# Three edits to a two-block fp32 kernel: the first mixture's loop written out on TensorE, the input rows on another queue, and zeros written elsewhere

## The reference

```python
def reference(x, ...):
    # first block, two layers
    x = x + even_mixer(rms_norm(x))       # differential attention beside a gated recurrence
    x = x + swiglu(rms_norm(x))           # dense, 2816 wide
    x = x + pool_mixer(rms_norm(x))
    x = x + moe_swiglu(rms_norm(x))       # "first mixture": 8 experts, 3584 wide, top 2 of 8
    x = rms_norm(x)
    # second block, one layer, with a context of 256 tokens
    x = x + mod[2] * hybrid_mixer(...)    # delta rule and gated linear attention, both directions
    x = x + mod[5] * hier_moe(...)        # "second mixture": 4 groups of 8 experts, 512 wide
    return rms_norm(x)

def moe_swiglu(t, ...):
    top_val, top_idx = top_k(t @ router_w, 2)
    gates = softmax(top_val)              # combine[:, e]: the gate of expert e, or 0
    for e in range(8):
        he = silu(t @ wg[e]) * (t @ wu[e])
        out = out + (combine[:, e:e + 1] * he) @ wd[e]
```

## Time and profile before

| | |
|---|---|
| median of 3 runs | 2699.87 us (2699.5 to 2700.07) |
| profiled execution, its own time | 2700.57 us |
| its span | 2698.8 us |
| TensorE matmul busy | 2468.5 us, 91% of the span |
| VectorE, ScalarE, GpSimd busy | 616.5, 379.6, 157.3 us |
| granted TensorE clock, mean | 0.963 of full speed |
| HBM read | 671.98 MB, 249 GB/s over the span |

### The profile page before, as it was taken

The page is one execution under the profiler, slowest core; times in us unless marked ns, Lnnn a source line. Parts: engine busy times, 40 slices in busy tenths (PEclk is TensorE's granted clock), DMA queues, the critical chain, the costliest instruction groups (busy, mean ns, idle before and its releaser), DMA issues.

```text
span 2698.8 us, 52755 instructions
## 1 busy us (share of the span) xinstructions
PE 2468.5 (91%) x24386; PEld 1591.9 (59%) x24386; DVE 616.5 (23%) x1160; ACT 379.6 (14%) x619; POOL 157.3 (6%) x145
## 2 busy tenths in 40 slices
PE   7778999799999999999999898899889889999997
PEld 5536776556556656655565678895567544444443
DVE  1451001201000000101010356741542232222223
ACT  1121101100000000000000333213241100000001
POOL 1000000000000000000000024520210000000000
PEclk9889999799999999999999999999999989999998
DMA  8484332599989999998999300022021459999995
GB/s 297 170 297 157 125 140 80 208 393 351 393 306 393 351 340 356 350 393 312 393 351 367 138 1 1 1 94 94 32 94 60 152 225 400 399 399 401 401 401 205
DMA packets 273260, 676.26 MB, mean 251 GB/s; under 512 B 5891, under 2 KB 9438, under 8 KB 268830
## 3 DMA queue, kind: packets, MB, share of 16 engines
q1 hardware_dynamic: 270624, 666.91, 65.7%
q0 software_dynamic: 2112, 6.04, 0.7%
q10 hardware_dynamic: 318, 0.10, 0.0%
HBM read 671.98 MB, written 1.05 MB: 249 GB/s over the span
## 4 chain that ended last, share of the span: by engine, by line
PE 76%; DMA 11%; DVE 6%; ACT 3%; issue 2%; SPq 2%; POOL 1%; DVEq 0%; ACTq 0%; POOLq 0%
PE ps L621 25%; PE ps L712 22%; PE ps L733 11%; DMA ring<-in_w_exp_up 10%; PE ps L797 5%; PE ps L965 3%; ACT arena L2017 2%; SPq L567 2%; PE ps L1098 1%; PE ps L1110 1%; PE ps L719 1%; PE ps L1108 1%; PE ps L695 1%; POOL arena L2475 1%; PE ps L944 1%
## 5 line engine op out<-in xcount | busy, mean ns | idle before, releaser
L712 PE MATMUL ps<-ring,arena 128*32 128x256 f32 x10752 | 598.0, 382 | 16.7 <-issue 15.4
L712 PEld LDWEIGHTS ps<-ring,arena 128*32 128x32 f32 x10752 | 349.0, 111 | 249.7 <-issue 32.1
L621 PE MATMUL ps<-hT,ring 128*128 128x256 f32 (+1 forms) x1792 | 443.1, 408 | 20.1 <-ACT arena L2017 7.3
L2017 ACT ACTIVATE arena<-ps 128x384 f32<-128x384 f32 (+5 forms) x312 | 165.9, 552 | 1830.0 <-PE ps L712 581.3
L621 PEld LDWEIGHTS ps<-hT,ring 128*128 128x128 f32 x1792 | 345.6, 193 | 121.1 <-issue 68.3
L733 PE MATMUL ps<-ring,arena 128*32 128x256 f32 x5376 | 300.5, 379 | 0.0
L797 PE MATMUL ps<-ring,arena 128*64 128x512 f32 x1024 | 233.8, 611 | 29.0 <-DMA ring<-in_w_exp_up 26.1
L733 PEld LDWEIGHTS ps<-ring,arena 128*32 128x32 f32 x5376 | 173.9, 110 | 115.3 <-issue 1.3
L1441 DVE TENSOR_TENSOR arena<-arena,ps 128x384 f32<-128x384 f32 x56 | 31.0, 554 | 825.2 <-ACT arena L2017 825.2
L797 PEld LDWEIGHTS ps<-ring,arena 128*64 128x64 f32 x1024 | 81.1, 141 | 178.5 <-issue 178.5
L621 PE MATMUL ps<-arena 128*128 128x128 f32 (+1 forms) x1064 | 133.7, 287 | 15.9 <-ACT arena L2017 5.1
(11 more groups left out here) (360 smaller groups left out, 1844.3 us busy)
## 6 DMA issues: line engine op xcount, KB each, us to landing
ring<-in_moe_wg SPq DMA_DIRECT2D x56, 2048.0 KB, 11.3
ring<-in_moe_wu SPq DMA_DIRECT2D x56, 2048.0 KB, 16.3
ring<-in_moe_wd SPq DMA_DIRECT2D x56, 2048.0 KB, 17.2
ring<-in_w_exp_gate SPq DMA_DIRECT2D x32, 2048.0 KB, 17.5
ring<-in_w_exp_up SPq DMA_DIRECT2D x32, 2048.0 KB, 18.8
ring<-in_w_exp_down SPq DMA_DIRECT2D x32, 2048.0 KB, 15.2
ring<-in_w_in SPq DMA_DIRECT2D x13, 2048.0 KB, 10.5
ring<-in_w_ada SPq DMA_DIRECT2D x12, 2048.0 KB, 10.5
```

Source lines behind the costliest of these rows:

```text
L621: last = mm(outp, l, r, start=(i == 0), stop=(i == n - 1))
L712: last = mm(flat[32 * q:32 * q + 32, S * r:S * r + S], x_[:, k, 32 * r:32 * r + 32], gu[:, :, k, q * P:(q + 1) * P], start=(k == 0), stop= ...
L2017: return nc.scalar.activation(*a, **k)
```

## The change

It has three parts.

1. The input's two token tiles are two DMAs at the head of SyncE's queue, each with a semaphore of its own, ahead of the first weights; ScalarE's first norm waits for tile 0 and tile 1 separately. GpSimd's queue begins with `table`.
2. In the first mixture's round that is always run, TensorE's loop over four passes is written out as eight experts, with constant semaphore values. The other engines' loops stay.
3. GpSimd zeroes `ysb` and `GcT` right after the linear attention's output is ready (`og_ready` 2), ahead of the wait for `res_ready` 6. `facc` is zeroed by ScalarE, as two copies of 128 x 1024 of `table` with scale 0, behind the copy of `frow`; VectorE waits for it before the second mixture's round.

```diff
--- before.py
+++ after.py
@@ -582,11 +582,14 @@
                         sp.wait_ge(*at("m2_dn", r * PAIRS + PAIRS))
                         sp.sem_inc(sem("rounds_streamed"), 1)
 
+            for t in range(NT):
+                sp.dma_start(res[:, t, :], ins["x"][0, t * P:(t + 1) * P, :]).then_inc(inc("x%d_in" % t), 16)
             before = [None] * NSLOT
             for i in range(len(plan)):
                 if i == 1:
                     sp.wait_ge(*at("rows_in", 16 * (len(ROWS_A) + len(ROWS_B))))
-                    sp.wait_ge(*at("x_in", 16))
+                    sp.wait_ge(*at("x0_in", 16))
+                    sp.wait_ge(*at("x1_in", 16))
                     sp.wait_ge(*at("table_in", 16))
                 load(i, before[i % NSLOT])
                 before[i % NSLOT] = plan[i][4]
@@ -747,9 +750,13 @@
                     down(U1 - 1)
 
                 gather(0, 0)
-                with pe.Fori(0, E1 // 2) as p:
-                    for b in range(2):
-                        expert(2 * p + b, b, R * UNITS + 2 * U1 * p + U1 * b, U1 * p)
+                if x == "m":
+                    for e in range(E1):
+                        expert(e, e % 2, U1 * e, U1 * (e // 2))
+                else:
+                    with pe.Fori(0, E1 // 2) as p:
+                        for b in range(2):
+                            expert(2 * p + b, b, R * UNITS + 2 * U1 * p + U1 * b, U1 * p)
                 scatter(E1, 0)
 
             def pairs_round(x, R):
@@ -1993,6 +2000,7 @@
             done(last)
             route(2, E2, C2, lgt, gprob)
             ve.wait_ge(*at("m2_zeroed", 1))
+            ve.wait_ge(*at("facc_zeroed", 1))
 
             def copy2(x_):
                 C = P
@@ -2134,7 +2142,7 @@
                 ac.dma_start(rowsB[o:o + n, :], v.rearrange("(r d) -> r d", d=P)).then_inc(inc("rows_in"), 16)
 
             functions(LN)
-            norm(0, res, [("x_in", 16)] * 2)
+            norm(0, res, [("x0_in", 16), ("x1_in", 16)])
             ac.wait_ge(*at("cols_ready", 1))
             gained(hTx, colA("ln_mix_even", 0, 8), "hT_act")
             ac.wait_ge(*at("lam_dot", 1))
@@ -2367,6 +2375,9 @@
             gained(hTx, gM, "hT_act", mod[:, 24:32, 0])
             ac.wait_ge(*at("grow_sum", 2))
             done(act(frow.rearrange("p (a b) -> p a b", a=2), ps[:, 4:6, :], ACT.Copy), "frow_ready")
+            for t in range(NT):
+                last = act(facc[:, t, :], table[:, 0:D], ACT.Copy, scale=0.0)
+            last.then_inc(inc("facc_zeroed"), 1)
             gdf = oh2[:, :, 0:4]
             ac.wait_ge(*at("grp_shift", 1))
             done(act(gdf, gdf, ACT.Exp), "grp_exp")
@@ -2379,7 +2390,6 @@
         @block.gpsimd
         def _(po):
             G = nc.gpsimd
-            po.dma_start(res[:, :, :], ins["x"][0].rearrange("(t p) d -> p t d", p=P)).then_inc(inc("x_in"), 16)
             po.dma_start(table[:, :], ins["k_table"]).then_inc(inc("table_in"), 16)
             po.dma_start(const1, ins["k_table1"]).then_inc(inc("table1_in"), 16)
             for i, name in enumerate(("lam_q1", "lam_q2", "lam_k1", "lam_k2")):
@@ -2475,15 +2485,15 @@
                     G.tensor_tensor(W2[l % 2].rearrange("p h (n c) -> p (h n) c", c=2 * b), g_, mid, ALU.subtract)\
                         .then_inc(inc("Wd_ready"), 1)
 
+            po.wait_ge(*at("og_ready", 2))
+            G.memset(ysb, 0.0)
+            G.memset(GcT[:, 1, :, :], 0.0).then_inc(inc("m2_zeroed"), 1)
             po.wait_ge(*at("res_ready", 6))
             with nc.allow_non_contiguous_dma(reason="router columns"):
                 po.dma_start(wre[:, :, 0:4], ins["w_router_grp_2"][0].rearrange("(k p) n -> p k n", p=P)).then_inc(inc("router2_in"), 16)
                 po.dma_start(wre[:, :, 4:36], ins["w_router_exp_2"][0].rearrange("(k p) n -> p k n", p=P)).then_inc(inc("router2_in"), 16)
             po.dma_start(brt[:, 0:4], ins["b_router_grp_2"].to_broadcast([P, 4])).then_inc(inc("router2_in"), 16)
             po.dma_start(brt[:, 4:36], ins["b_router_exp_2"].to_broadcast([P, 32])).then_inc(inc("router2_in"), 16)
-            G.memset(facc, 0.0)
-            G.memset(ysb, 0.0)
-            G.memset(GcT[:, 1, :, :], 0.0).then_inc(inc("m2_zeroed"), 1)
             po.dma_start(glrow, ins["g_final_2"][None, :].to_broadcast([P, D])).then_inc(inc("glrow_in"), 16)
```

## The result

The changed kernel takes 2681.31 us (median of 4 runs, 2678.46 to 2682.54), the kernel before in the same comparison 2699.97 (4 runs, 2699.5 to 2700.84). The ratio is 0.9929, 95% interval 0.9912 to 0.9946: faster by 18.7 us. The forecast was 2675.1 with a range of 2672.4 to 2678.8, so the sign was right and the time 6 us too low, outside the range. The profiled execution after took 2680.94 us, with a span of 2679.1 (before: 2698.8). All of the following differences are taken between these two spans, which are 19.7 us apart.

The account below looks back on a forecast made before the run. TensorE's matmuls were taken to bound the kernel (76% of the chain of waits, DMA 11%). Loop 22.3, start 2.2 and zeros 0.3 us made 24.8 us off 2699.87: forecast 2675.1 us, range 2672.4 to 2678.8.

Parts of the forecast that it names:

- the loop's term: First mixture, TensorE's loop written out: 15.4 us idle plus 6.9 us at the low clock, 22.3 us gained.
- As after the change TensorE has no gap there to cool in: First mixture: the first groups of experts 3, 5 and 7 run at 10.36 us, gaining 6.9 us.
- C: First mixture: the wait at the turn isn't the branch's but belongs to each second expert; 2697.4 us, chance 0.05.
- D: First mixture: TensorE's code, four times as long, is fetched too late in the straight run; up to 2709.9 us, chance 0.03.
- E: First mixture: another engine's loop keeps part of the turn, a third of 22.3 us stays; 2682.5 us, chance 0.04.
- the start: Input rows first on SyncE's queue: the norm starts 2.41 us earlier; 2.2 us taken, between 1.8 and 2.4.
- Rival B: Kernel start gives nothing, as x lands near 11.5 or the table or small rows come late; 2677.3 us, chance 0.12.
- the zeros: Second router: without memsets transposes start 2.3 us earlier, but TensorE waits for router DMAs; 0.3 us gained, ends 0 and 2.3.
- of the 2.3 us 0.2 are left, and with the matmuls' own lead-in 0.3: Second router: TensorE, there at 2154.7, waits till 2156.75 for the last router DMA, leaving 0.3 us gain.
- rival A: Second router: the router columns don't bind, so the memsets' whole 2.3 us come in; 2673.1 us, chance 0.12.
- the sum: Whole kernel: 22.3 + 2.2 + 0.3 = 24.8 us less than the median 2699.87, forecast 2675.1 us.
- a microsecond taken from TensorE's path counts: Whole kernel: outside the second mixture's loads DMA binds only the very start, so TensorE savings shorten the total.

Follow-up runs that it names:

- The two versions with the early columns: Zeros moved and the second router's four column and bias DMAs issued some 100 us earlier: on the kernel before 2697.49 us, on the changed kernel 2675.38 us.

## Why the prediction missed

**Right: the loop's term.** 22.3 us were forecast for the mixture, 22.29 came, in the changed kernel and with the loop alone. That each branch back costs TensorE some 5 us was confirmed by putting branches back: 5.22, 5.31, and 5.17 and 5.23 us of idle time, each ahead of the expert where the branch was put. "As after the change TensorE has no gap there to cool in" held within the mixture. Rivals C, D and E fall: the wait belongs to the branch, and the straight code shows no wait above 1.1 us in 970 us. That fits the rule of the Trainium skill, Runtime: NRT & Kernel Launch, section Instruction fetch mechanics, that code is prefetched in sequence and a taken branch out of it waits; the runs show the branch's price, not the fetch itself.

**Right within what the runs can tell: the start.** 2.2 us forecast; 2.23 at the transposes in the pair of profiles, 1.8 on average at the first square over all fifteen, 2.2 in the medians with this part alone, whose interval has no change in it. The close agreement of the pair is in part luck, since the 11.57 that the term starts from is the latest of four. Rival B falls: in all eleven profiles with the edit x was there by 9.39.

**Half right: the zeros.** VectorE's 0.75 us, the wait for the bias and the transposes came as forecast. The step "of the 2.3 us 0.2 are left, and with the matmuls' own lead-in 0.3" failed: it took the matmuls behind the wait at 3.66 us, their time without a wait in front. They took 4.54, and the low clock went on behind them. The term is not +0.3 but -0.5 between the first two profiles, -2.3 in the changed kernel's second profile and -2.5 us in the medians by itself. Its lower end, 0, was no bound: a wait that takes the place of a busy stretch can cost more than it hides. The two versions with the early columns show that the bias was the cause, and rival A would have been right only with them.

**Wrong: the sum.** The step that failed is the one that was never written as a term, that a microsecond won up to the mixture's end is won at the end ("a microsecond taken from TensorE's path counts", "so this carries on"): the stages behind were put at nothing. The lead was 24.40 us at the mixture's end, as summed, and 19.25 us ahead of the second router. 1.0 went in the k projection, 3.3 in the narrow matmuls, the transposes and the first q chains, 0.8 in the delta rule up to the second router. These were matmuls at 1.2 GHz that had run at 2.4. By place: 2.11 + 22.29 - 1.03 - 2.20 - 0.17 - 0.91 - 0.95 + 0.12 - 0.52 + 0.97 = 19.71 us, the difference of the spans. (-1.03 to -0.91 are the four pieces with what lies between them, -0.95 and +0.12 lie between the last row and 2094.54, -0.52 is the second router, +0.97 the second mixture.) These places are those of one execution: the second one lost 1.1 us up to the last row, 0.9 from there to the second router and 2.3 in it. The stated range does not follow from its own ends either: 23, 2.4 and A's 2.3 us give 2672.2, and 20 with nothing for the start and the zeros 2679.9. The result lies outside both.

The twelve profiles with the matmul order of the changed kernel sort as follows. With no turn in the mixture (five profiles of three kernels) the low stretch around the narrow matmuls is 10.2 to 13.7 us long, and 1.0 to 4.3 us are lost between the mixture's end and the last row. With two or three turns, and with one ahead of the seventh expert, the stretch is 6.8 us in all six. With one turn ahead of the fifth it is 13.6. So the loop written out brings this loss with it. The k projection goes either way: 16.07 to 16.32 us in the six with the short stretch, 17.06 to 17.10 in four of the others, 15.54 and 15.45 in two.

What decides it stays open. My first theory, that any gap in the mixture does it, fell with the turn ahead of the fifth expert. The last gap alone is enough, but two earlier ones are too, the later of which ends at 1002 us, where the single one that ends at 993 did nothing. The time at 1.2 GHz within the mixture would sort them as well (0 and 3.4 us: long; 6.8 and more: short), which was not varied by itself.

The traces show another sign that sorts all twelve: how soon the clock falls in TensorE's wait ahead of the k projection. The stretch from 6.6 to 7.9 us behind the start of the mixture's last group (L695 before, L698 after), for the kernel before, the changed one, and those with one turn ahead of the fifth and of the seventh expert:

```profile
1501.05:1502.35 1.30, 0.00 (x0) 0.00 (x0) 0.00 (x0) 1.30 (x3) 0.00 (x0) 0.50 1.01 372
```

```profile
1476.66:1477.96 1.30, 0.00 (x0) 0.00 (x0) 0.00 (x0) 1.30 (x3) 0.00 (x0) 1.00 1.03 381
```

```profile
1482.72:1484.02 1.30, 0.00 (x0) 0.00 (x0) 0.00 (x0) 1.30 (x3) 0.00 (x0) 1.00 1.01 370
```

```profile
1483.34:1484.64 1.30, 0.00 (x0) 0.00 (x0) 0.00 (x0) 1.30 (x3) 0.00 (x0) 0.50 1.03 373
```

TensorE is idle in all four. In the six profiles with the short stretch the clock has fallen 6.0 to 6.5 us behind that start, in the six others only 8.0 to 8.2 us behind it. The turn ahead of the fifth expert made the mixture 6.70 us longer and left this at 8.0; the one ahead of the seventh made it 8.38 us longer and moved it to 6.5. So the turns may matter only by how far they shift the program against the clock's falls, and not as gaps. Even the plain time of arrival sorts the profiles: long where that last group starts by 1476.12, short where it starts at 1476.74 or later. The earlier start of the input rows alone left the 6.0 as it was, and no run moves the clock's fall against the program other than through the turns. So these readings are not told apart.

Nor did the pieces' gain reach the end in the two kernels that had it: with one turn at the old place the median was 2687.5, against 2682 to 2683 expected, and with two it was 2693.2, against 2690, as the low stretches around the second router grew. So it is not shown that the 5 us could be had back. Taking the narrow matmuls' own low stretch away did not pay either: VectorE's way to `gdec` is the next limit there.

## What to carry to other kernels

A loop on TensorE with a body of thousands of instructions cost about 5 us here at each turn, plus 1.5 to 3.1 us in the group behind it at the low clock; it shows as idle time with "issue" as releaser ahead of the body's first line, and writing it out gave it back in full up to the loop's end. When a gain comes from gaps taken out, price the stretches of narrow or small matmuls behind them at both levels of the clock, and put a loss on the list; here a sum over removed waits was an upper end. One profile of each kernel does not say where a loss lies: profile the same program twice before a piece of 1 to 2 us is explained. When work is moved to free an engine, look for the DMA that was just hidden and issue it earlier in the same edit: here that turned a loss of 2.5 us into a gain of 3.6.

## What the runs showed of the hardware

- The granted clock fell to 1.2 GHz with TensorE busy without a pause, in narrow matmuls (128 x 16) behind wide ones: 0.51 over 14 us, with the engine busy for all of them, in the kernel with the loop alone (1548 to 1562). With four of them behind each wide one it stayed at full speed (1.00 from 1540 to 1550, with the engine as busy).
- How long it stayed low there changed with an edit hundreds of microseconds ahead of it: 6.8 or 10.2 to 13.7 us for the same instructions.
- The bias rows, a DMA of 16 KB on GpSimd's queue, landed after 9.9 us beside weight loads at 261 to 464 GB/s and after 3.1 us when all queues together moved 29 GB/s.
- A branch taken on TensorE cost 5.05 to 5.31 us of idle time, sixteen of them in seven kernels, whether the body had two experts or four.
